# Inverting sixteen triangular matrices: the transposed inverse from a PE transpose and a ScalarE copy instead of a product and a VectorE subtraction

## The reference, cut to what matters

```python
def step(state, inp):
    r_t, w_t, k_t, v_t, kk_t, a_t = inp
    s_kk = jnp.einsum('bhvk,bhk->bhv', state, kk_t)
    state = (state * w_t[:, :, None, :]
             - s_kk[..., None] * (kk_t * a_t)[:, :, None, :]
             + v_t[..., None] * k_t[:, :, None, :])
    y_t = jnp.einsum('bhvk,bhk->bhv', state, r_t)
    return state, y_t
```

## Time and profile before

| what | value |
|---|---|
| three runs | 2083.54 us median (2080.19 to 2083.65) |
| the profiled execution's own time | 2078.96 us |
| its span, first to last instruction | 2077.1 us |
| mean granted TensorE clock | 0.959 of full speed |
| busy over the span | PE 95%, DVE 57%, ACT 42%, POOL 3% |
| stage of the 24 steps | about 1113 to 1179.5 us from the span's start |

### The profile page before, as it was taken

The page is one execution under the profiler, slowest core; times in us unless marked ns, Lnnn a source line. Parts: engine busy times, 40 slices in busy tenths (PEclk is TensorE's granted clock), DMA queues, the critical chain, the costliest instruction groups (busy, mean ns, idle before and its releaser), DMA issues.

```text
span 2077.1 us, 23954 instructions
## 1 busy us (share of the span) xinstructions
PE 1968.3 (95%) x9946; PEld 1647.4 (79%) x9946; DVE 1181.6 (57%) x1397; ACT 870.7 (42%) x1089; POOL 60.3 (3%) x138
## 2 busy tenths in 40 slices
PE   6999999799999997999998979999999899999998
PEld 6987768678888886888888967888788788667887
DVE  4314353478888896554358834555545459455454
ACT  4313330267767774443221153444444345324443
POOL 0020000000000000000000000000000000210000
PEclk9989999899999999999998999999999989679999
DMA  8332223469898995545230005555555344007551
GB/s 341 140 120 102 95 88 142 168 236 371 329 354 330 345 358 208 182 183 182 102 122 21 1 1 223 183 182 186 199 183 183 142 162 144 19 1 272 182 182 41
DMA packets 51226, 363.74 MB, mean 175 GB/s; under 512 B 5680, under 2 KB 5808, under 8 KB 8496
## 3 DMA queue, kind: packets, MB, share of 16 engines
q1 hardware_dynamic: 50976, 360.13, 46.8%
q10 hardware_dynamic: 144, 2.10, 0.3%
HBM read 361.15 MB, written 1.05 MB: 174 GB/s over the span
## 4 chain that ended last, share of the span: by engine, by line
PE 88%; DVE 6%; ACT 3%; issue 1%; DMA 0%; POOL 0%; SPq 0%; POOLq 0%; DVEq 0%; ACTq 0%
PE bank L2041 8%; PE bank L2418 8%; PE bank L2420 7%; PE bank L2419 7%; PE bank L1987 7%; PE bank L2253 4%; PE bank L2445 4%; PE bank L2443 4%; PE bank L2444 4%; PE bank L2314 3%; PE bank L2316 3%; PE bank L2315 3%; PE bank L2243 3%; PE bank L2329 2%; PE bank L2331 2%; PE bank L2330 2%
## 5 line engine op out<-in xcount | busy, mean ns | idle before, releaser
L1220 DVE TENSOR_TENSOR w_a<-ring,w_a 128x2048 fp32r<-128x2048 f32 x221 | 504.5, 2290 | 303.4 <-ACT w_a L771 303.0
L771 ACT ACTIVATE w_a<-ring 128x2048 fp32r<-128x2048 f32 x221 | 420.6, 1912 | 162.7 <-PE bank L2445 90.7
L2418 PE MATMUL bank<-w_a,h 128*128 128x512 f32 x536 | 214.4, 400 | 11.1 <-DVE h L1275 5.6
L2420 PE MATMUL bank<-w_a,h 128*128 128x512 f32 x536 | 210.2, 392 | 0.0
L2419 PE MATMUL bank<-w_a,h 128*128 128x512 f32 x536 | 209.8, 391 | 0.0
L2041 PE MATMUL bank<-H,ring 128*128 128x256 f32 x800 | 182.7, 385 | 0.0
L1220 DVE TENSOR_TENSOR w_b<-ring,w_b 128x2048 fp32r<-128x2048 f32 x62 | 142.0, 2291 | 66.2 <-ACT w_b L771 65.6
L2041 PEld LDWEIGHTS bank<-H,ring 128*128 128x128 f32 x800 | 151.3, 192 | 26.0 <-issue 5.8
L1987 PE MATMUL bank<-h,w_a 128*128 128x256 f32 x1152 | 144.9, 288 | 7.0 <-DVE h L1275 7.0
L1987 PEld LDWEIGHTS bank<-h,w_a 128*128 128x128 f32 x1152 | 141.4, 194 | 11.1 <-DVE h L1275 7.4
L771 ACT ACTIVATE w_b<-ring 128x2048 fp32r<-128x2048 f32 x62 | 118.7, 1914 | 45.7 <-PE bank L2445 25.7
(11 more groups left out here) (455 smaller groups left out, 3292.5 us busy)
## 6 DMA issues: line engine op xcount, KB each, us to landing
ring<-in_stream SPq DMA_DIRECT2D x330, 1024.0 KB, 4.9
G<-in_gains SPq DMA_DIRECT2D x15, 512.0 KB, 5.8
arena<-in_cmp_w ACTq DMA_DIRECT2D x1, 2048.0 KB, 7.9
sm<-in_small SPq DMA_DIRECT2D x1, 1582.0 KB, 12.9
con<-in_consts SPq DMA_DIRECT2D x1, 1384.0 KB, 17.7
X<-in_x SPq DMA_DIRECT2D x2, 512.0 KB, 3.9
out_x<-X SPq DMA_DIRECT2D x2, 512.0 KB, 2.6
sm<-in_small SPq DMA_DIRECT2D x1, 666.5 KB, 22.7
```

The costliest lines, as they stand in the source:

```text
L771: act.activation(w_slot(unit)[:, 0, :], ring[:, unit % RING, :], ACT.Copy).then_inc(S("w_hi"), 1)
L1220: dve.tensor_tensor(w_slot(unit)[:, 1, :], ring[:, unit % RING, :], w_slot(unit)[:, 0, :].bitcast(FP32), ALU.subtract).then_inc(S("w_lo"), 1)
L2418: pe.matmul(bank[4 + t][:, :], x_hi, w[0][:, k, :], start=first, stop=False)
L2420: ins = pe.matmul(bank[4 + t][:, :], x_lo, w[0][:, k, :], start=False, stop=end)
```

## The change

W is no longer updated by products and a subtraction of its own. It is made from the new M: after `mw_out(n)` four PE transposes write M^T into bank 5 or 6 (`w_in`), and ScalarE copies the bank into `mat_w`. VectorE's subtraction on W and the `Q^T W` products go. New semaphores are `w_full` (transposes done) and `w_turned` (copy done). `w_in(n-2)` stands behind `mw_in(n-1)` on TensorE, for the first 20 steps. Nothing else in the program is edited; lines below the edits shift by four and then by two more.

```diff
             make_diags(DIAGS)
+            for n in range(N_INV - 4):
+                act.wait_ge(S("w_full"), n + 1)
+                act.activation(mat_w[:, 4 * (n % 4):4 * (n % 4) + 4, :], tiles(bank[5 + n % 2][:, :], 4), ACT.Copy)\
+                   .then_inc(S("w_turned"), 1)
...
                 dve.wait_ge(S("mw_full"), n + 1)
-                if n < N_INV - 4:
-                    dve.tensor_tensor(mat_w[:, four, :], mat_w[:, four, :], tiles(bank[5 + n % 2][:, :], 4), ALU.subtract)
                 dve.tensor_tensor(mat_m[:, four, :], mat_m[:, four, :], tiles(bank[2 + n % 2][:, :], 4), ALU.subtract)\
                    .then_inc(S("mw_ok"), 1)
...
             def mw_in(n):
                 g = n % 4
                 pe.wait_ge(S("q_ok"), n + 1)
+                if n >= 4:
+                    pe.wait_ge(S("w_turned"), n - 3)
                 if n >= 2:
                     pe.wait_ge(S("mw_ok"), n - 1)
                 for i in range(4):
                     q = mat_q[:, n % 2, i * P:(i + 1) * P]
                     ins = pe.matmul(bank[2 + n % 2][:, i * P:(i + 1) * P], mat_w[:, 4 * g + i, :], q, start=True, stop=True)
-                    if n < N_INV - 4:
-                        ins = pe.matmul(bank[5 + n % 2][:, i * P:(i + 1) * P], q, mat_w[:, 4 * g + i, :], start=True,
-                                        stop=True)
                 ins.then_inc(S("mw_full"), 1)
+
+            def w_in(n):
+                pe.wait_ge(S("mw_ok"), n + 1)
+                if n >= 2:
+                    pe.wait_ge(S("w_turned"), n - 1)
+                for i in range(4):
+                    ins = pe.transpose(bank[5 + n % 2][:, i * P:(i + 1) * P], mat_m[:, 4 * (n % 4) + i, :], C("ident"))
+                ins.then_inc(S("w_full"), 1)
...
                     q_in(n)
                 if n:
                     mw_in(n - 1)
+                if 2 <= n < N_INV - 2:
+                    w_in(n - 2)
```

## The result

The changed kernel takes 2069.76 us (median of 4 runs, 2067.79 to 2070.84) against 2083.22 us before (4 runs, 2080.19 to 2083.65): ratio 0.9943, 95% interval 0.9925 to 0.996. Ratios are given as they are on record; the quotient of the two medians here would be 0.9935. Forecast were 2072.8 us, range 2066.5 to 2078.5. The forecast of 10.7 us less is a ratio of 0.9949, inside both intervals. The changed kernel's profiled execution took 2068.77 us, with a span of 2067.0.

The account below looks back on a forecast made before the run. TensorE and VectorE were taken as tied within 0.03 us per step. TensorE-led steps of 2.23 us instead of 2.68 end the stage at 1168.8, not 1179.53: 2083.54 - 10.7 = 2072.8 us, range 2066.5 to 2078.5.

Parts of the forecast that it names:

- The tie: In the 24 inversion steps, TensorE's 2.68 us and VectorE's 2.70 us per step were tied within 0.03 us.
- The price of a transpose: On TensorE in the steps, one record of 0.11 us per transpose, against 0.22 for a product.
- the 8.9 worked out: Rival in the steps: transposes cost what products do, 80 x 0.1117 = 8.9 us back, 2081.7 us; chance 3%.
- VectorE's and ScalarE's room: Per step of 2.23 us, VectorE needs 2.11, leaving 0.12; ScalarE's copy of 0.60 to 0.65 us costs nothing.
- the rival of a slower VectorE: In the steps, ScalarE working alongside slows VectorE to 2.46 us a step, 4.6 us back, 2077.4 us; chance 5%.
- Added waits: TensorE's new waits in the steps are met in time: 5.4 us against 1.0, 4.0 against 1.0, and 1.2 slack.
- The sum: Over the inversion stage, its terms put the first product with the inverses at 1168.8 instead of 1179.53, gain 10.7 us.
- The 19 steps: Iterations 3 to 21 on TensorE, 20 records each at 0.1117 us: 42.4 us, to 1162.4.
- their end: After the 19 steps, TensorE's last 1.79 us, then VectorE's 4.4 us, from 1162.4 to the stage's end at 1168.8.
- Passed on: Work after the inversion starts earlier by the same amount, so 10.7 us counts in full; rival of losing it 5%.
- The rule on the clock: Rival in the steps: transposes don't count as activity, clock stays low, 31 us slower, 2115 us; chance 4%.
- the attention rows: Attention stage with 48 transposes, clock at 0.50 while PE reads 10.00 of 10; cited for the low-clock rival.

Follow-up runs that it names:

- the two half changes: VectorE instead of ScalarE copying in the changed kernel: 2079.96 us, ratio 1.0; kernel before without VectorE's subtraction from W: 2081.04 us, ratio 1.0.
- Identity products: The changed kernel with the inversion's four transposes a step made as fp32 products with the identity: 2081.77 us, ratio 1.0003 to before.
- the second profile: The changed kernel measured again, unedited, in five rounds beside the kernel before: 2071.47 us, ratio 0.9954 (0.9937 to 0.9972).

## Why the prediction was right

*The tie.* "A removal on one engine alone would bring next to nothing": shown by the two half changes, 1.5 us each.

*The price of a transpose*: 0.11 us, taken from another stage, held: 4 in 0.44 us in all 20 steps. Identity products gave the gain back, a little more (9.3 to 9.7 us) than the 8.9 worked out.

*VectorE's and ScalarE's room.* The masking takes 691 ns as before, the subtraction from M 687 (median) where it was 680, with ScalarE copying beside them; the rival of a slower VectorE falls. Added waits never held TensorE up, even with ScalarE's path twice as long.

*The sum* was 10.7 us for the stage, and it measured 11.84 in the first profile and 11.41 in the second. The largest part that was off is the time at the low clock. I had copied 5.9 us after `mw_in(0)` from the earlier trace rows. In the changed kernel the third group of eight records takes 1.08 us, which is 1.8 records at 0.2137 and 6.2 at 0.1117: the rise comes 4.2 us after `mw_in(0)`. With the same working it comes after 5.1 us in the second profile (third group 1.51) and after 5.4 with the copies doubled (1.67), and the stages follow: 53.73, 54.16 and 54.32 us, towards the 54.9 of the sum. Each us at the low clock costs 0.48 us of time, since 0.1117 is 0.52 of 0.2137. So 0.2 to 0.8 us of these gains are the clock's and not the change's: that much of the outcome was luck, and a forecast should carry it in its range.

The other 0.3 us of the first profile's difference come from elsewhere. The 19 steps took 42.2 us for 42.4, and their end 6.2 for 6.4. The sum also gave the first product after the pause no extra time, where `mw_in(0)` takes 2.08 us and the next eight records 1.71, 0.37 more; and it took two records too many at the low clock, 0.21. These two slips work against each other.

*Passed on*: 61.7 us from the inverses to the output projection before, 62.1 after, and 0.4 us less over everything behind the inversion. The totals agree only within their scatter: 9.6 us by the second ratio for 11.4 in its stage.

*The rule on the clock.* The prediction names the wrong page for it: it stands in the Trainium skill, TensorE: Matmul & The Clock Gate, Part 4: PE-mode transpose, and says that a transpose doesn't count as TensorE activity as a matmul does; the times that it gives there are for bf16. The runs don't bear that out for this kernel's fp32 transposes: with sixteen transposes of 32 records in a step the clock stayed at 1.00, and in the attention stage it rose early with more transposes. What holds it down there stays open. I gave it 4% on the strength of the earlier trace rows; the attention rows, which looked like evidence for it, were not.

## What to carry to other kernels

When two engines have steps of equal length, count what an edit takes from each; only the smaller saving arrives, and half an edit measured as nothing here. A product kept only to have a result transposed can be a transpose and a copy: in fp32 it cost TensorE half as much here, and the evacuation went to the engine that slept. If a replacement experiment raises the clock, run the control that adds the same number of records of the old kind before believing in the kind.

## What the runs showed of the hardware that was not expected

In the attention stage more work on TensorE went with a faster stage. With 48 records more (each transpose repeated, or made as a product of two records) it took 52.5 to 54.1 us in five profiles instead of 61.9 to 63.1 in nine, since the granted clock rose from 0.50 to 1.00 early in it. Why is not shown.

The time from the end of TensorE's pause to the rise of its clock also varied between executions of nearly the same code: 5.9 us after `mw_in(0)` in the kernel before, 4.2 in the first profile of the changed kernel, and 5.1 to 5.5 in the nine other profiles that begin the steps in this way.
